# A 2-block transformer kernel: the first w_ada rows in three chunks, partly on TensorE, and four smaller moves

## The chip, the cores and the metric

The kernel runs on one core of a Trainium2 chip. The metric is the time of one execution on the device in microseconds (us), lower is better. A core has TensorE (PE), VectorE (DVE), ScalarE (ACT), GpSimd (POOL) and SyncE (SP); each has an instruction queue of its own, they meet by semaphores, and DMA queues move data between HBM and SBUF. Nearly all loads are issued by SP, in the order of its program.

## What is computed

The reference is two blocks, 256 tokens by 2048 features, in float32. What the change touches is the start of the first block and its three uses of the vector `mod`:

```python
c_act = jax.nn.silu(c)
mod = c_act @ w_ada[l] + b_ada[l]                 # 2048 x 12288
sh1, sc1, gt1, sh2, sc2, gt2 = jnp.split(mod, 6, axis=-1)
h = modulate(rms_norm(x, g_mix[l]), sh1, sc1)     # h * (1 + sc1) + sh1
z = h @ w_in[l]                                   # projections of both attentions, gates
...
x = x + gt1[:, None, :] * (merged @ w_out[l])
h = modulate(rms_norm(x, g_ffn[l]), sh2, sc2)
...
x = x + gt2[:, None, :] * y
```

`w_ada` has 100 MB. Only one token of `c` goes through it, so it is read once and never reused. The indexer of the second attention scores each key for each query over 16 heads of 64, and a top-64 picks keys. A second block (gated linear attention, SwiGLU) and the last norm follow.

## The kernel before

The kernel is written by hand, engine by engine, and the order on each queue is the order of the program. Every large product is made from **halves**: two k-tiles (256 rows) by 512 columns of a weight, 512 KB, loaded by SP into one of eight places of `raw`. ScalarE copies a half rounded to fp32r into one of four places of `whi` (L1041), VectorE subtracts and writes the rest into `wlo` (L1617), and TensorE does twelve matmuls with it (L499 to L501: high by high, high by low part of the weight, low part of the activation by high). `split` and `half` are these steps; `body` on ScalarE and VectorE runs ahead of TensorE by up to four halves, and small steps hang on it as hooks by the index of a half: after the split of that half, in order.

**Stage A** is the first 112 halves, 14 groups of 512 columns of `z`. It needs sh1 and sc1 per feature. Features come in 16 k-tiles; a pair of k-tiles feeds one half. The first six k-tiles (`EARLY`) are made before stage A: 16 row pieces of `w_ada` (128 rows by 2 x 768 columns, 768 KB each, `early_piece`, L329) are loaded into six slots; VectorE multiplies each by its column of `cact` = silu(c) and adds it to `acc0` (`early_add`, L1700). TensorE then sums over the 128 partitions by narrow matmuls with ones (`first_columns`, L577), in two chunks of columns (`CHUNKS`), VectorE makes `gs_mix` and `sh_mix` from that (`first_modulation`), and ScalarE and VectorE scale the transposed x and split it into `hi` and `lo` (`first_high`, `first_affine`, `first_low`, `first_pair`). x itself is loaded after four row pieces (L358); its root mean square is made on ScalarE and VectorE, its rows are scaled on ScalarE (L1074), and TensorE transposes them in eight pairs (`turn`, L524, L533). While TensorE would wait, `keep_running` gives it matmuls that nothing uses (L589).

Stage A runs over all 14 groups with the first three pairs, and then over them again with the other five. The last ten k-tiles come from 32 late pieces (640 KB, `late_piece`, L336), one after each half 4 to 35 in SP's queue; VectorE adds them (`late_add`, L1721), and after half 38 (`LATE_SUMMED`) 20 narrow matmuls sum them (L583). The pairs are made at `LATE_PAIRS`. All halves of `w_in` are loaded after all early pieces. Small vectors (later parameters, the bias table) are loaded after early piece 9 and transposed by TensorE before stage A (L572, L575).

The rest of `w_ada` is loaded in 128 chunks between later halves and added on VectorE (`ada_add`). Two of its results, the gates gt1 and gt2, are rows: `ada_rows` (L553) sums `ada_acc` over partitions and spreads it by four matmuls of float32 ones, once in stage U, once at the end of the first FFN. VectorE adds the bias (`modulation_row`).

In stages O, U, F1e, GQ, GO and F2p TensorE transposes eight pairs each between halves, one pair after a half (`turn`), and ScalarE and VectorE split each (`plain_pair`, `scaled_pair`, `held_pair`). In stage C1 the index heads run between halves: `ix_turn` of pair p after half 3p, `ix_scores` after half 3p + 2 (L687 to L710).

Of the kernel before, what the change touches and what calls it, by code (L numbers as in the profile page):

```python
# [5 lines left out]
P = 128  # L6
S = 256
TB = S // P
D = 2048
# [51 lines left out]
CHUNKS = ((0, 2), (2, EARLY), (EARLY, KT))  # L61
EARLY_ROWS = KT + 1
# [5 lines left out]
A_HELD = 3  # L68
A_ENDS = [A_FIRST + (KT // 2 - A_PAIRS) * (n + 1) for n in range(GROUPS)]
A_HALVES = [(g, p) for g in A_GROUPS for p in range(A_PAIRS)] + [(g, p) for g in A_AGAIN for p in range(A_PAIRS, KT // 2)]  # L70
LATE_SUMMED = 38
LATE_PAIRS = 41
# [19 lines left out]
def build_program(nc, A, out):  # L92
# [22 lines left out]
    ada0 = at("ada0", [P, SLOTS, 2 * EARLY * P], ARENA)  # L115
# [40 lines left out]
    gt_row1 = at("gt_row1", [P, D], ARENA + 48 * KB)  # L156
    xT1 = at("xT1", [P, KT, S], ARENA + 24 * KB)
# [96 lines left out]
    csg = small[:, 96:112]  # L254
    ss, ssy = small[:, 112:114], small[:, 114:116]
# [43 lines left out]
    def _(sp):  # L299
# [64 lines left out]
        for i in range(A_ENDS[-1]):  # L364
            first_half(i)
            if RING <= i < RING + 2 * KT:
                late_piece(i - RING)
            if i == 2 * RING:
                sp.wait_ge(sem("erow_held"), 1)
                sp.dma_start(e_dram, erow[:]).then_inc(sem("e_out"), 16)  # L370
# [111 lines left out]
    def _(pe):  # L482
# [23 lines left out]
        def group(it, phase, per, gper, idx0, gi, n, hooks, kt0=0, x_hi=hi, x_lo=lo, lead=None, parts=None, ready=None, ahead=4, made=None, by_block=None):  # L506
# [4 lines left out]
            for i in range(n):  # L511
# [8 lines left out]
                if lead is not None and i < 8 - ahead:  # L520
                    turn(lead, ahead + i, ready and (ready, (ahead + i) // 2 + 1))
                hooks(idx0 + i)

        def turn(src, g, ready=None):  # L524
# [11 lines left out]
            pairs[0] += 1  # L536

# [28 lines left out]
        pe.wait_ge(sem("xs_made"), 2)  # L566
        for g in range(KT // 2):
            turn(X, g)
        pe.wait_ge(sem("tt_free"), KT // 2)
        pe.wait_ge(sem("par_in"), 8 * 16)  # L570
        for n, rws in ((1, 120), (2, 116)):
            m = pe.transpose(aux[2][:, n % 2 * P:n % 2 * P + rws], parr[0:rws, n, :], ident[0:rws, 0:rws])  # L572
        m.then_inc(sem("par_T"), 1)
        pe.wait_ge(sem("rel_in"), 32)
        pe.matmul(aux[3][0:NH, :], relb[:], onehot[:], start=True, stop=True).then_inc(sem("par_T"), 1)  # L575

        def first_columns(n):  # L577

            k0, k1 = CHUNKS[n]
            acc, c0, w, wide = (acc1, 0, KT - EARLY, WIDE // 4) if n == 2 else (acc0, k0 * P, k1 - k0, WIDE // 2)  # L580
            for j in range(2 * w):
                c = c0 + j % w * P
                m = pe.matmul(aux[n % 2][:, j * wide:(j + 1) * wide], acc[:, j // w, c:c + P], ones[:, 0:wide], start=True, stop=True)  # L583
# [7 lines left out]
        pe.wait_ge(sem("ada0_sum"), KT - 3)  # L591
        keep_running(3)
        pe.wait_ge(sem("ada0_sum"), KT - 1)
        keep_running(1)
        for kc in range(2):
            pe.wait_ge(sem("ada0_sum"), KT + kc)
            first_columns(kc)
        keep_running(1)
        pe.wait_ge(sem("par_cols"), 2)
        pe.wait_ge(sem("erow_held"), 1)  # L600
# [18 lines left out]
        def sb_turn(h):  # L619
# [5 lines left out]
            pe.wait_ge(free0, 2 + GROUPS - A_HELD + (2 if h < NH // 2 else 5))  # L625
            pe.wait_ge(free1, 2 + GROUPS - A_HELD + (2 if h < NH // 2 else 5))
# [18 lines left out]
        def sb_values(h):  # L645
            pe.wait_ge(sem("sb_a"), h + 1)
            pe.wait_ge(sem("head_out"), h)
            if h == 0:
                pe.wait_ge(free0, 2 + GROUPS - A_HELD + 3)
                pe.wait_ge(free1, 2 + GROUPS - A_HELD + 3)  # L650
# [4 lines left out]
        for i, (g, p) in enumerate(A_HALVES):  # L655
            again = i >= A_FIRST
            n = (i - A_FIRST) // (KT // 2 - A_PAIRS) if again else i // A_PAIRS
            held = n < A_HELD if again else n >= GROUPS - A_HELD
            banks = first_banks[(GROUPS - A_HELD + n) % 3] if again and held else lin[n % 2] if again else first_banks[n % 3]
            if p == (A_PAIRS if again else 0) and not (again and held):  # L660
                pe.wait_ge(free0, 12 + n if again else n)
                pe.wait_ge(free1, 12 + n if again else n)
            if n == 0:
                pe.wait_ge(sem("tt_lo"), p + 1)
            half(0, "A", A_ENDS[-1], i, 0, 2 * p, p == (0 if held or not again else A_PAIRS), p == (KT // 2 - 1 if held or again else A_PAIRS - 1),
                 banks=banks)
            if i == LATE_SUMMED:
                pe.wait_ge(sem("ada0_sum"), EARLY_ROWS + 2 * KT)
                first_columns(2)
            if i == A_ENDS[0] - 1:  # L670
                project_ix()
            if i == A_ENDS[0] + 2:
# [92 lines left out]
        def o_hooks(it):  # L765
            def run(idx):
# [3 lines left out]
                if c >= 0 and step < 2:  # L770
                    if c == 0 and step == 0:
                        pe.wait_ge(sem("head_out"), 2 * NH)
                    turn(merged, 2 * c + step, (sem("og_add1"), c + 1))
# [5 lines left out]
        def last_merged(idx):  # L779

            if idx in (2, 3):
                turn(merged, 4 + idx, (sem("og_add1"), 4))
# [1837 lines left out]
```

## Time and profile before

| | us |
|---|---|
| median of three runs (2665.74 to 2667.66) | 2667.6 |
| the profiled execution | 2666.06 |
| its span, first to last instruction | 2664.2 |
| TensorE busy | 2625.6 |
| first projection matmul starts at | 48.21 |

The span is what the profile shows of one execution; all rows below come from it. The page gives busy time by engine, the span in slices, the DMA queues and the chain of waits that ended last; the timeline gives single instructions in order of time. TensorE being busy means that its pipeline holds a matmul; the distance from one start to the next says how fast it goes.

### The profile page before, as it was taken

To read this page: it belongs to the slowest core of one execution; us is meant where nothing else is said; L and a number is where in the kernel's file an instruction comes from. 1 tells how busy PE (TensorE), PEld (TensorE's weight loads), DVE (VectorE), ACT (ScalarE), POOL (GpSimd) and SP (SyncE) were. 2 spreads that over 40 slices of the span, in tenths; PEclk is the share of its full clock that TensorE was granted. 3 is DMA by queue.
4 is the path that set the end of the run, shared out by engine and by line. 5 is a ranking of instruction groups with operands and counts; after the bars stand their busy time and mean duration, and the time that the engine had idled before them with its cause. 6 is when DMAs were issued, how large, how long until landed. Compare 5 with 4: busy or idle time off the path is not lost.

```text
span 2664.2 us, 33329 instructions
## 1 busy us (share of the span) xinstructions
PE 2625.6 (99%) x12045; PEld 2164.4 (81%) x12045; DVE 1798.2 (67%) x2072; ACT 1297.8 (49%) x1574; POOL 230.2 (9%) x164
## 2 busy tenths in 40 slices
PE   5999999999999999999999999999999999999999
PEld 3888887888888888888888887887888888888887
DVE  7978777878776677776766855677555555555554
ACT  4455544455454444444444554556454444444443
POOL 0000000100000000000001210240001111111110
PEclk9999999999999999999999999999999999999999
DMA  9989768678867766666665666644666666666663
GB/s 382 401 308 340 243 209 281 196 237 283 304 211 241 220 220 219 218 218 216 218 195 177 198 178 181 190 143 132 199 186 193 190 189 189 190 190 191 191 191 134
DMA packets 280792, 585.61 MB, mean 220 GB/s; under 512 B 22033, under 2 KB 24493, under 8 KB 279797
## 3 DMA queue, kind: packets, MB, share of 16 engines
q1 hardware_dynamic: 280340, 583.61, 68.1%
q8 instruction: 58, 0.95, 0.1%
q10 hardware_dynamic: 352, 0.71, 0.1%
q14 instruction: 42, 0.34, 0.0%
HBM read 582.07 MB, written 2.11 MB: 219 GB/s over the span
## 4 chain that ended last, share of the span: by engine, by line
PE 96%; DVE 2%; DMA 1%; ACT 0%; issue 0%; DVEq 0%; ACTq 0%
PE lin L499 30%; PE lin L501 30%; PE lin L500 30%; DMA sb_ada<-in_w_ada_dram 1%; PE aux L812 1%; PE aux L499 1%; PE aux L501 1%; PE aux L500 1%; PE aux L533 1%; PE aux L986 0%; PE aux L823 0%; DVE sb_wlo L1617 0%; DVE sb_acc L1708 0%; PE aux L557 0%; PE aux L999 0%
## 5 line engine op out<-in xcount | busy, mean ns | idle before, releaser
L1617 DVE TENSOR_TENSOR sb_wlo<-sb_raw,sb_whi 128x1024 fp32r<-128x1024 f32 x896 | 1114.8, 1247 | 784.8 <-ACT sb_whi L1041 781.2
L1041 ACT ACTIVATE sb_whi<-sb_raw 128x1024 fp32r<-128x1024 f32 x896 | 948.9, 1060 | 1237.2 <-PE lin L501 1159.1
L499 PE MATMUL lin<-sb_whi,sb_act_hi 128*128 128x512 f32 x2620 | 1038.4, 396 | 1.9 <-DVE sb_wlo L1617 1.0
L501 PE MATMUL lin<-sb_whi,sb_act_lo 128*128 128x512 f32 x2620 | 1021.8, 390 | 0.0
L500 PE MATMUL lin<-sb_wlo,sb_act_hi 128*128 128x512 f32 x2620 | 1020.7, 390 | 0.0
L499 PEld LDWEIGHTS lin<-sb_whi,sb_act_hi 128*128 128x128 f32 x2620 | 492.5, 188 | 108.5 <-issue 9.3
L501 PEld LDWEIGHTS lin<-sb_whi,sb_act_lo 128*128 128x128 f32 x2620 | 492.1, 188 | 104.3
L500 PEld LDWEIGHTS lin<-sb_wlo,sb_act_hi 128*128 128x128 f32 x2620 | 492.7, 188 | 99.9 <-issue 1.9
L499 PE MATMUL lin<-sb_whi,sb_hid_hi 128*128 128x512 f32 x704 | 275.3, 391 | 0.0
L501 PE MATMUL lin<-sb_whi,sb_hid_lo 128*128 128x512 f32 x704 | 274.1, 389 | 0.0
L500 PE MATMUL lin<-sb_wlo,sb_hid_hi 128*128 128x512 f32 x704 | 274.0, 389 | 0.0
L501 PEld LDWEIGHTS lin<-sb_whi,sb_hid_lo 128*128 128x128 f32 x704 | 132.1, 188 | 27.6
L499 PEld LDWEIGHTS lin<-sb_whi,sb_hid_hi 128*128 128x128 f32 x704 | 132.2, 188 | 27.0
L500 PEld LDWEIGHTS lin<-sb_wlo,sb_hid_hi 128*128 128x128 f32 x704 | 132.2, 188 | 26.9
L1636 DVE SCALAR_TENSOR_TENSOR sb_ada_acc<-sb_ada_in,sb_small,sb_ada_acc 128x1024 f32<-128x1024 f32 x90 | 119.0, 1322 | 0.9 <-DVE sb_u_lo L1686 0.9
L2505 POOL TENSOR_TENSOR sb_yacc<-sb_yacc,sb_dstage 128x512 f32<-128x512 f32 x36 | 57.2, 1590 | 555.4 <-ACT sb_dstage L1055 555.4
L2505 POOL TENSOR_TENSOR sb_x<-sb_x,sb_dstage 128x512 f32<-128x512 f32 x36 | 63.6, 1766 | 336.2 <-ACT sb_dstage L1055 336.2
L2484 POOL TENSOR_TENSOR sb_hank<-sb_hank,sb_selneg 128x384 f32<-128x384 f32 x8 | 11.6, 1491 | 496.2 <-DVE sb_selneg L1895 496.2
L2511 POOL TENSOR_TENSOR sb_ubuf<-sb_ubuf,sb_cacc 128x512 f32<-128x512 f32 x11 | 18.1, 1648 | 397.4 <-ACT sb_ubuf L1055 397.4
L499 PE MATMUL lin<-sb_whi,sb_u_hi 128*128 128x512 f32 x128 | 51.0, 398 | 0.0
L501 PE MATMUL lin<-sb_whi,sb_u_lo 128*128 128x512 f32 x128 | 49.9, 390 | 0.0
L500 PE MATMUL lin<-sb_wlo,sb_u_hi 128*128 128x512 f32 x128 | 49.9, 390 | 0.0
(362 smaller groups left out, 1819.5 us busy)
## 6 DMA issues: line engine op xcount, KB each, us to landing
sb_raw<-in_w_in_dram SPq DMA_DIRECT2D x176, 512.0 KB, 6.7
sb_raw<-in_ffn_w_gu_dram SPq DMA_DIRECT2D x176, 512.0 KB, 3.7
sb_ada_in<-in_w_ada_dram SPq DMA_DIRECT2D x128, 512.0 KB, 5.1
sb_raw<-in_gla_w_in_dram SPq DMA_DIRECT2D x96, 512.0 KB, 3.8
sb_raw<-in_w_gate_dram SPq DMA_DIRECT2D x88, 512.0 KB, 3.8
sb_raw<-in_w_up_dram SPq DMA_DIRECT2D x88, 512.0 KB, 4.4
sb_raw<-in_w_down_dram SPq DMA_DIRECT2D x88, 512.0 KB, 4.4
sb_raw<-in_ffn_w_down_dram SPq DMA_DIRECT2D x88, 512.0 KB, 3.6
```

Of the source, the lines that this page charges most:

```text
L499: pe.matmul(o, h, whi[:, w], start=first and q == 0, stop=False)
L500: pe.matmul(o, h, wlo[:, w], start=False, stop=False)
L501: m = pe.matmul(o, l, whi[:, w], start=False, stop=last and q == 1)
L533: m = pe.transpose(aux[n % 4][:, q * S + tb * P:q * S + (tb + 1) * P], src[:, tb, (2 * g + q) * P:(2 * g + q + 1) * P], ident)
L812: m = pe.transpose(aux[f // 2][:, f % 2 * S + tb * P:f % 2 * S + (tb + 1) * P], src[:, tb, f * P:(f + 1) * P], ident)
L1041: act.activation(whi[:, idx % RING * HALF:(idx % RING + 1) * HALF], raw[:, idx // 2 % RING, idx % 2 * HALF:(idx % 2 + 1) * HALF], ACT.Copy ...
L1617: dve.tensor_tensor(wlo[:, c], raw[:, idx // 2 % RING, idx % 2 * HALF:(idx % 2 + 1) * HALF], whi[:, c].bitcast(fp32), ALU.subtract).then_i ...
L1636: dve.scalar_tensor_tensor(acc[:, c], ada_in[place][:], cact[:, kt:kt + 1], acc[:, c], ALU.mult, ALU.add).then_inc(sem("ada_sum"), 1)
L2484: pool.tensor_tensor(hank[:, h, :], hank[:, h, :], selneg[:], ALU.add).then_inc(sem("bias_made"), 1)
L2505: pool.tensor_tensor(y[:, 0, s], y[:, 0, s], dstage[:, c % 2, :], ALU.add).then_inc(sem("dstage_free"), 1)
L2511: pool.tensor_tensor(ubuf[:, 0, :], ubuf[:, 0, :], cacc[:].rearrange("p a t -> p (a t)")[:, 0:NB], ALU.mult).then_inc(sem("up_mul"), 1)
```

## The change

It does five things.

1. The early rows come in three chunks of two k-tiles: 48 row pieces of 128 rows by 2 x 256 columns (256 KB, rows of 1 KB), in six slots. 25 of them are multiplied by TensorE itself (`row_columns`: four matmuls with a column of `cact`, summed in PSUM), 23 are added by VectorE (`row_add`) and brought in by `chunk_columns`. x is loaded first of all; its scaling is shared by ScalarE and VectorE. The pieces of chunks two and three stand in SP's queue between the first halves (`PIECES_FROM`), and their takers between the first halves of TensorE (`ROWS_BEHIND`) and VectorE (`ADDS_AT`). Piece n waits until row n - 6 is taken. The first nine halves go by pair (three groups with pair 0, then with pair 1, then with pair 2). Late pieces stand after halves 7 to 38, and the late sums after half 39. The fillers before stage A are gone.
2. The later parameters are loaded after half 8 and transposed after half 12 of stage A.
3. The gate rows: `ada_acc` is split by ScalarE (`gate_high`) and VectorE (`gate_low`) into two fp32r parts; `ada_rows` makes eight fp32r matmuls.
4. `turn_two` turns two pairs after one half where two halves had one pair each.
5. `ix_scores` of pair p comes with `ix_turn` of pair p + 1, one half later.

The core of the diff:

```diff
+ROW_PIECES = 3 * KT
+TENSOR_ROWS = [n for n in range(KT) if n % 3 != 2] + list(range(KT + 1, 2 * KT, 2)) + [33, 36, 39, 42, 45, 47]
+VECTOR_ROWS = [n for n in range(ROW_PIECES) if n not in TENSOR_ROWS]
+ROWS_BEHIND = {0: (17, 19), 1: (21, 23), 2: (25, 27), 3: (29, 31), 4: (33,), 5: (36,), 6: (39, 42, 45, 47)}
+ADDS_AT = {0: (16, 18), 1: (20, 22), 2: (24, 26, 28, 30), 3: (32,), 4: (34, 35), 5: (37, 38, 40, 41), 6: (43, 44, 46)}
+PIECES_FROM = (0, 8, 16, 24, 32, 37, 42, 48)
+LATE_FROM = 7
-LATE_SUMMED = 38
-LATE_PAIRS = 41
+LATE_SUMMED = 39
+LATE_PAIRS = 42
...
+        def row_piece(n):
+
+            if n >= SLOTS:
+                row_taken(n - SLOTS)
+            kt, c = n % KT, n // KT
+            sp.dma_start(ada0[:, n % SLOTS, :].rearrange("p (b n) -> p b n", b=2), w_first[kt * P:(kt + 1) * P, :, 2 * c * P:2 * (c + 1) * P]
+                         ).then_inc(sem(f"ada0_in{n % SLOTS}"), 16)
+
+        def row_taken(n):
+
+            if n in TENSOR_ROWS:
+                sp.wait_ge(sem("ada0_T"), row_on_tensor(n))
+            else:
+                sp.wait_ge(sem("ada0_sum"), VECTOR_ROWS.index(n) + 1)
...
+        sp.dma_start(X[:], tokens(A["x"][0])).then_inc(sem("x_in"), 16)
+        for n in range(PIECES_FROM[1]):
+            row_piece(n)
+        for i in range(A_ENDS[-1]):
+            first_half(i)
+            if i + 2 < len(PIECES_FROM):
+                for n in range(PIECES_FROM[i + 1], PIECES_FROM[i + 2]):
+                    row_piece(n)
+            if i == 8:
                 for n, r, src in later_loads:
...
+        def row_columns(n):
+
+            kt, c = n % KT, n // KT
+            pe.wait_ge(sem(f"ada0_in{n % SLOTS}"), 16 * (n // SLOTS) + 16)
+            if all(m >= n for m in TENSOR_ROWS if m // KT == c):
+                pe.matmul(column_banks[c][:, 0:4], ident, nothing, start=True, stop=False)
+            for j in range(4):
+                m = pe.matmul(column_banks[c][:, j:j + 1], ada0[:, n % SLOTS, j * P:(j + 1) * P], cact[:, kt:kt + 1], start=False, stop=False)
+            m.then_inc(sem("ada0_T"), 1)
+
+        def chunk_columns(c):
+
+            pe.wait_ge(sem("ada0_sum"), sum(n < (c + 1) * KT for n in VECTOR_ROWS))
+            for j in range(4):
+                b, k = j // 2, 2 * c + j % 2
+                m = pe.matmul(column_banks[c][:, j:j + 1], acc0[:, b, k * P:(k + 1) * P], ones[:, 0:1], start=False, stop=j == 3)
+            m.then_inc(sem("ada0_T"), 1)
...
+        pe.wait_ge(sem("csg_made"), 2)
+        for n in TENSOR_ROWS[:8]:
+            row_columns(n)
         pe.wait_ge(sem("xs_made"), 2)
         for g in range(KT // 2):
             turn(X, g)
+            if g in (1, 3, 5):
+                row_columns(TENSOR_ROWS[8 + g // 2])
+        chunk_columns(0)
...
+        for i, (g, p, a, first, last) in enumerate(A_HALVES):
...
+            for n in ROWS_BEHIND.get(i, ()):
+                row_columns(n)
+            if i in (A_HELD, 2 * A_HELD):
+                chunk_columns(i // A_HELD)
+            if p == made:
+                made += 1
+                pe.wait_ge(sem("tt_lo"), made)
+            half(0, "A", A_ENDS[-1], i, 0, 2 * p, first, last, banks=banks)
+            if i == 12:
+                late_parameters()
...
         def ada_rows(n):
-            pe.wait_ge(sem("ada_sum"), 64 * (n - 1))
+            pe.wait_ge(sem("mod_made"), 2 * n - 1)
             for j in range(4):
-                m = pe.matmul(aux[j][:], ones, ada_acc[:, j * NB:(j + 1) * NB], start=True, stop=True)
+                c = slice(j * NB, (j + 1) * NB)
+                pe.matmul(aux[j][:], ones_r[:], (gt_hi1, gt_hi)[n - 2][:, c], start=True, stop=False)
+                m = pe.matmul(aux[j][:], ones_r[:], gt_lo[:, c], start=False, stop=True)
...
         def ix_hooks(idx):
-            p, step = idx // 3, idx % 3
-            if p < NIX // 2 and step == 0:
+            p = idx // 3
+            if idx % 3 == 0 and 1 <= p <= NIX // 2:
+                ix_scores(p - 1, p - 1)
+            if idx % 3 == 0 and p < NIX // 2:
                 ix_turn(p, p)
-            if p < NIX // 2 and step == 2:
-                ix_scores(p, p)
...
+        row_add(2)
+        row_add(5)
+        norm_stats(0)
+        dve.tensor_scalar(X[:, 1, :], X[:, 1, :], rstd[:, 1:2], None, ALU.mult).then_inc(sem("xs_made"), 1)
+        for n in (8, 11, 14):
+            row_add(n)
...
+        def early_pair(g):
+            first_modulation(g)
+            dve.wait_ge(sem("gs_made"), g + 1)
+            if g < 2:
+                first_affine(g)
+            first_low(g, xaff[:, g, :, :] if g < 2 else xT[:, 2 * g:2 * g + 2, :])
...
+        for g in range(A_PAIRS):
+            hk.setdefault(A_HELD * g, []).append(lambda g=g: early_pair(g))
+        for i, adds in ADDS_AT.items():
+            for n in adds:
+                hk.setdefault(i, []).insert(len(hk.get(i, ())) - (i == 6), lambda n=n: row_add(n))
...
+            act.activation((gt_hi if n else gt_hi1)[:], ada_acc[:], ACT.Copy).then_inc(sem("mod_made"), 1)
...
+            dve.tensor_tensor(gt_lo[:], ada_acc[:], (gt_hi if n else gt_hi1)[:].bitcast(fp32), ALU.subtract).then_inc(sem("mod_made"), 1)
```

## Rows read from the trace of the kernel before

**Rows 1.** The page: busy time by engine; the chain that ended last, by engine.
```profile
PE 2625.6 (99%) x12045; PEld 2164.4 (81%) x12045; DVE 1798.2 (67%) x2072; ACT 1297.8 (49%) x1574; POOL 230.2 (9%) x164
...
PE 96%; DVE 2%; DMA 1%; ACT 0%; issue 0%; DVEq 0%; ACTq 0%
```

**Rows 2.** Timeline of TensorE, stage A: start us, us, engine, line, operation, out<-in, count.
```profile
30.33 5.57 PE L533 MATMUL aux<-sb_con,sb_x 128*128 128x128 f32 x32 [20.52 <-ACT sb_x L1074]
...
48.21 0.47 PE L499 MATMUL lin<-sb_whi,sb_act_hi 128*128 128x512 f32 x1 [0.32 <-DVE sb_act_lo L1752]
...
130.06 0.47 PE L499 MATMUL lin<-sb_whi,sb_act_hi 128*128 128x512 f32 x1
...
147.68 0.47 PE L499 MATMUL lin<-sb_whi,sb_act_hi 128*128 128x512 f32 x1
...
155.94 4.53 PE L583 MATMUL aux<-sb_con,sb_acc 128*128 128x16 f32 x40
...
160.72 0.63 PE L500 MATMUL lin<-sb_wlo,sb_act_hi 128*128 128x512 f32 x1
...
164.05 0.40 PE L499 MATMUL lin<-sb_whi,sb_act_hi 128*128 128x512 f32 x1
```

**Rows 3.** Windows: stretch, length, busy us of PE, PEld, DVE, ACT, POOL, clock, DMA, GB/s.
```profile
10.00:30.00 20.00, 0.00 (x0) 0.00 (x0) 16.08 (x13) 9.41 (x9) 0.00 (x0) 1.00 1.03 401
...
120.00:140.00 20.00, 20.00 (x86) 15.61 (x85) 18.51 (x14) 9.79 (x13) 0.00 (x0) 1.00 1.04 402
...
161.00:165.00 4.00, 4.00 (x13) 3.09 (x13) 1.92 (x2) 3.94 (x7) 0.00 (x0) 0.63 0.71 244
```

**Rows 4.** Waits in 48 to 165 us: us in total, times, longest.
```profile
ACT sb_whi L1041 <- DMA sb_raw<-in_w_in_dram: 46.5, 29, 2.1
```

**Rows 5.** Timeline of ScalarE in the head.
```profile
18.03 1.91 ACT L1062 ACTIVATE sb_junk<-sb_x 128x2048 f32<-128x2048 f32 x1 [7.65 <-DMA sb_x<-in_x_dram]
...
22.09 1.28 ACT L1069 ACT_TABLE_LOAD   x1
...
26.29 3.90 ACT L1074 ACTIVATE sb_x<-sb_x,sb_small 128x2048 f32<-128x2048 f32 x2 [0.23 <-DVE sb_small L1677]
```

**Rows 6.** Timeline of VectorE, its first add.
```profile
10.93 1.02 DVE L1705 TENSOR_SCALAR sb_acc<-sb_ada,sb_small 128x1536 f32<-128x1536 f32 x1 [0.27 <-DVEq L1698]
```

**Rows 7.** Groups by form, 0 to 48 us: busy us, mean ns, idle before.
```profile
L1041 ACT ACTIVATE sb_whi<-sb_raw 128x1024 fp32r<-128x1024 f32 x2 | 2.1, 1049 | 5.2 <-DMA sb_raw<-in_w_in_dram 5.2
...
L1617 DVE TENSOR_TENSOR sb_wlo<-sb_raw,sb_whi 128x1024 fp32r<-128x1024 f32 x1 | 1.2, 1224 | 0.0
L1116 ACT ACTIVATE sb_act_hi<-sb_xT,sb_small 128x256 fp32r<-128x256 f32 x2 | 1.1, 593 | 0.0
...
L1718 DVE SCALAR_TENSOR_TENSOR sb_acc<-sb_ada,sb_small,sb_acc 128x512 f32<-128x512 f32 x1 | 0.8, 752 | 0.1
```

**Rows 8.** DMA issues: out<-in, KB each, median us to landing (second FFN; output stores).
```profile
sb_raw<-in_ffn_w_down_dram SPq DMA_DIRECT2D x77, 512.0 KB, 3.6
...
out_dram<-sb_x SPq DMA_DIRECT2D x2, 256.0 KB, 2.3
```

**Rows 9.** Timeline of SP's queue in the head, two rows of its issues.
```profile
0.75 2.17 SPq L333 DMA_DIRECT2D sb_ada<-in_w_ada_dram  x4
...
18.17 0.56 SPq L361 DMA_DIRECT2D sb_parr<-in_b_ada_dram  x1
...
22.97 9.38 SPq L333 DMA_DIRECT2D sb_ada<-in_w_ada_dram  x6
```

**Rows 10.** Timeline of TensorE: the half behind a turn, and a gate row.
```profile
627.12 0.47 PE L499 MATMUL lin<-sb_whi,sb_act_hi 128*128 128x512 f32 x1
627.43 0.39 PE L500 MATMUL lin<-sb_wlo,sb_act_hi 128*128 128x512 f32 x1
...
706.80 3.59 PE L557 MATMUL aux<-sb_ada_acc,sb_con 128*128 128x512 f32 x8
```

**Rows 11.** Timeline of ScalarE in stage U: a split and the idle time before it.
```profile
692.49 1.06 ACT L1041 ACTIVATE sb_whi<-sb_raw 128x1024 fp32r<-128x1024 f32 x1 [1.66 <-PE lin L501]
```

More of the change, by code:

```diff
@@ L254, in build_program @@
     csg = small[:, 96:112]
+    nothing = small[:, 184:188]
     ss, ssy = small[:, 112:114], small[:, 114:116]
@@ L519, in group @@
                 half(it, phase, per, idx0 + i, gi, kt0 + 2 * i, i == 0, i == n - 1, x_hi, x_lo, by_block=by_block if i == n - 1 else None)
-                if lead is not None and i < 8 - ahead:
-                    turn(lead, ahead + i, ready and (ready, (ahead + i) // 2 + 1))
+                if lead is not None and i < 8 - ahead and i % at_once == 0:
+                    for g in range(ahead + i, ahead + i + at_once):
+                        turn(lead, g, ready and (ready, g // 2 + 1))
                 hooks(idx0 + i)
@@ L536, in turn, with turn_two @@
             pairs[0] += 1
+        def turn_two(src, g, ready=None):
+            for n in range(2):
+                turn(src, g + n, ready)
         def ada_columns(part):
@@ L565, in _, with late_columns @@
         pe.wait_ge(sem("par_cols"), 1)
[L566 to L583, printed above, removed]
+        column_banks = (lin[0][1], aux[0], aux[1], aux[1])
+        def row_columns(n):
[12 more added lines that the diff above has]
+            m.then_inc(sem("ada0_T"), 1)
+        def late_columns():
+            pe.wait_ge(sem("ada0_sum"), EARLY_ROWS + 2 * KT)
+            pe.wait_ge(sem("par_cols"), 2)
+            pe.wait_ge(sem("erow_held"), 1)
+            for j in range(2 * LATE):
+                c = j % LATE * P
+                m = pe.matmul(aux[1][:, j * (WIDE // 4):(j + 1) * (WIDE // 4)], acc1[:, j // LATE, c:c + P], ones[:, 0:WIDE // 4], start=True, stop=True)
             m.then_inc(sem("ada0_T"), 1)
@@ L654, in _ @@
         first_banks = (lin[1], lin[0], aux[2:4])
[L655 to L666, printed above, removed]
+        made = 0
+        for i, (g, p, a, first, last) in enumerate(A_HALVES):
+            n = a - A_DRAINS
+            banks = lin[n % 2] if n >= A_HELD else first_banks[a % 3]
+            if first and a >= 3:
+                pe.wait_ge(free0, A_DRAINS + 1 + n if n >= A_HELD else a)
+                pe.wait_ge(free1, A_DRAINS + 1 + n if n >= A_HELD else a)
+            for n in ROWS_BEHIND.get(i, ()):
[8 more added lines that the diff above has]
+                late_parameters()
             if i == LATE_SUMMED:
-                pe.wait_ge(sem("ada0_sum"), EARLY_ROWS + 2 * KT)
-                first_columns(2)
-            if i == A_ENDS[0] - 1:
+                late_columns()
+            if i == A_ENDS[0]:
                 project_ix()
-            if i == A_ENDS[0] + 2:
+            if i == A_ENDS[0] + 3:
                 wix_turn()
@@ L873, in at_end @@
                     pe.wait_ge(sem("gpad_made"), FB)
-                if idx in range(24, 28) and n == 0:
-                    turn(X, idx - 24, (sem("x_made"), (idx - 24) // 2 + 1))
+                if idx in (24, 26) and n == 0:
+                    turn_two(X, idx - 24, (sem("x_made"), (idx - 24) // 2 + 1))
             for k in range(2):
```

233 lines of the change are left out of this document (115 added, 118 removed).

## The prediction

> **What bounds the kernel now.** The page first: TensorE is busy for 99% of the span and 96% of the chain that ended last is its matmuls [rows 1]. So a change gains only where TensorE waits, or where its own work shrinks. The timeline of TensorE shows the one long wait: the first projection matmul starts at 48.21 [rows 2]. From there halves (12 matmuls, two k-tiles by 512 columns) follow without a gap: 30 halves up to 130.06, 2.72 us each. Half 36 starts at 147.68, and the 39th ends at 155.94, where the late columns begin; 39 times 2.72 would end at 154.3, so 1.7 us are lost in between.
>
> The windows say why [rows 3]: from 10 us to 140 us the DMA queues carry some 400 GB/s without a break. The waits say it again: ScalarE's splits wait 46.5 us in 29 pieces for `sb_raw` [rows 4]. So the head has two limits at once, the late start of TensorE and a full DMA queue. A half needs 0.52 MB, a late piece 0.66 MB; both together take 2.95 us at 402 GB/s, more than the 2.72 us of a half. The lead of the old order (eight halves loaded before TensorE starts) is used up by half 30.
>
> **The first rows, up to the first half.** x goes to the head of SP's queue. It landed at 18.03 behind 3.1 MB of rows [rows 5]; without them (7.9 us at 400 GB/s) about 10.1. Squares took 4.1, the table load 1.28 [rows 5], root, reciprocal and hand-overs 0.6; the scaling is shared by ScalarE and VectorE, 2.0 instead of 3.9. Rows of x are scaled at 18.3. TensorE however has eight rows of w_ada ahead of the transposes. A row is four narrow matmuls; the late columns are 20 of them, 40 records in 4.37 us [rows 2], so 0.87 a row. The first can start at 10.9, when silu(c) is there [rows 6]. Rows 0, 1, 3 and 4 are taken by 14.7; row 10's piece waits for row 4 (six slots), and lands behind pieces 6 to 9 and half 0 at about 19.3. Transposes start at 20.2; they took 5.6 [rows 2], three rows between them 2.6, the last copy 0.6 (somewhat over half of a split's 1.05): 29.0. Then the split of half 0 on ScalarE 1.05 and VectorE 1.2, the modulation 0.45, the high part 1.05, the low part 0.65 (half of VectorE's 1.2) [rows 7], hand-overs 0.4: first half at T0 = 33.8, 14.4 us earlier than before.
>
> **Halves 0 to 6: where I expect the time to go.** SP's queue is in order, and each row piece now waits for the row six earlier to be taken. Many of these takers stand behind a projection step: on VectorE behind a split, on TensorE behind a half. The halves' own loads stand in the same queue behind these waits. One load, from issue to landing, is 3.6 for 512 KB with little queued [rows 8]; for 256 KB I take 3.0, that less 0.6 for the bytes (ends: 2.3, the 256 KB stores of [rows 8], and 3.6). An issue is 0.5 [rows 9], a VectorE add of 512 columns 0.75 [rows 7]. In us from T0:
> - Row 16 is added after the first pair's modulation, at 0.2; only then are pieces 22 and 23 and half 2 issued. Row 23 lands at 4.0, so TensorE starts half 1 at 4.9, and after rows 25 and 27 half 2 at 9.4.
> - Piece 31 waits for row 25 (8.5), half 3 is behind it, lands at 13.2; split 2.3, modulation, high and low 2.5: half 3 at 18.0, though half 2 ended at 12.1.
> - Pieces 39 to 41 wait for row 33, which TensorE takes after half 3 (21.6); half 5 is behind them, lands 5.7 later and is split at 29.6: half 5 at 29.8, half 4 having ended at 24.3.
> - Piece 45 waits for row 39, taken after half 5 (33.4); pieces 46, 47 and half 6 are behind it: landed 39.1, split 41.4, three adds 43.5, column sums 44.8, modulation, first pair (1.7 on ScalarE), low: half 6 at 47.9.
>
> So half 6 starts at 81.7, against 48.21 + 6 x 2.72 = 64.5 before. DMA carries little meanwhile: about 19 MB by the time half 6 has landed (73 us), where the old order had carried 28.
>
> **The clock.** After the late columns the next eight matmuls came 0.43 apart instead of 0.23 until 164.05 [rows 2]: 1.2 GHz instead of 2.4 (granted clock 0.63 in that window [rows 3]), 1.7 us lost, with nothing before but narrow matmuls. Halves 0, 3, 5 and 6 start after narrow matmuls and a wait, and the fillers that ran ahead of half 0 are gone. If all four start low, the steps above come to 52.8 from T0 (half 0's loss is partly behind row 23's landing), half 6 itself losing 1.7 more. Without any loss it is 47.9; the row is nearest to a loss, but of 4.4 us of narrow matmuls. I take about a third of it.
>
> **From half 6 to the late columns.** Half 6's load is issued 12.8 ahead of half 6, at 69 us, and from there the queue can stay full: halves 6 to 39 and 32 late pieces are 38.8 MB, 96.5 us, so half 39 lands at 168, before TensorE wants it (171.5): no stall. TensorE does 34 halves (92.5), and the later parameters, moved from a hidden place into its stream after half 12: two transposes and one matmul, 1.3. Their ten small loads (4.8 of SP's time [rows 9]) now stand after half 8, ahead of late piece 1, which waits for row 43 anyway; that piece and the others move three halves back, which costs what the sum holds. The store of the bias row moves to half 32, far ahead of its reader. Late columns start at 175.5 without clock losses, 182.1 with all. Before, after 40 halves, they would be at 155.94 + 2.72 = 158.7. That is 16.8 to 23.4 us lost. One half less stands between the late columns and the first late pair (two halves, 5.4 us); modulation, pair and low part need about 3, so they stay hidden.
>
> **Gate rows.** Four matmuls in two passes each, 8 records in 3.4 us, twice [rows 10]. Eight fp32r matmuls of 512 columns at 0.23 each are 1.8: 1.6 saved, twice, 3.2. The split into high (ScalarE, 2.0, by the 2048-column copies of [rows 5]) and low (VectorE, 2.4, two of the 1.2 of [rows 7]) lies two halves ahead of its use, where ScalarE idles 1.66 per half [rows 11]. Behind them stand a split and two pairs on each engine, which are due a half later than they come; without that cover up to 4.4 each would show. No new DMA.
>
> **Two pairs at a time, index scores.** After a turn the first spacing is 0.31 instead of 0.23 [rows 10]; every break that goes saves that 0.08 or nothing. 15 turns and 8 index scores: 0 to 1.8, I take 1.3. The scores come one half later, and so do relu, sums and mask on ScalarE and VectorE; the eight top-8 steps end at the same half as before, so the attention that waits for them does not move.
>
> **The sum.** +16.8 +2.2 (a third of the clock) -0.5 (between the ends of the landing) -3.2 -1.3 = +14.0 on the profiled execution's 2666.06 (span 2664.2): 2680. That execution is 1.5 below the median of 2667.6, within 0.06%. With all waits short (256 KB at 2.3, T0 at 32, no clock loss) it is about 2672; with all clock losses 2685, with a landing of 3.6 near 2689.
>
> **A rule of the skill.** By the rows a 256 KB piece lands after about 3.0 [rows 8], estimated. The Trainium skill (DMA: Bandwidth & Descriptors, Rules for kernel authors) asks for 1 MiB or more per DMA, which speaks against pieces of a third of the old size; its fit (Anatomy of one DMA) of 2.0 us and bytes over 436 GB/s would make 2.6 of the 3.0, an estimate, and with four such landings on the chain the sum 1.6 lower, 2678. No row here shows a load of 256 KB alone.
>
> **Rivals.**
> 1. The queue stays full (faster). If takers are always ahead of the pieces, DMA sets the end as it did: half 36 was gated at 147.68; three more halves are 1.6 MB, 3.9 us, so half 39 runs at 151.6, and the late columns start at 154.3, 4.4 earlier than before's 158.7. With the gate rows and the breaks 2657. It decides if the queue never runs dry before half 6, that is if half 6 starts by about 62. For it: T0 plus 40 halves plus 14 rows is also 154. Against it: the order of the takers in the code, above all rows 33 and 39. Chance 0.13.
> 2. Only one of the stalls shows (no change). If halves 3 and 5 are not held up (10 us less) and only half 6 waits, with no clock loss: 2668. Chance 0.12.
> 3. My forecast, 2672 to 2688. 0.68.
> 4. More than that: 1 KB rows slower than the 2 KB ones, or a wait in the gate rows that shows; 2688 to 2695. 0.07.
> That the change doesn't do what it says is unlikely: each step is in the diff.
>
> About 0.2% (5.3 us) is what a measurement of this kernel can tell from no change. Faster is rival 1, 0.13; same rival 2, 0.12; slower the rest, 0.75. The range, 2664 to 2690, leaves out rival 1 and the far end of 4. The slower cases alone lie at 2672 to 2690.
>
> **What would show it.** Right: first half at 31 to 35; TensorE idle before halves 3 and 5 for 4 to 6 us each and before half 6 for over 10; DMA in 30 to 75 us well under 400 GB/s; SP waiting for `sb_ada` rows there; late columns at 172 to 183; gate rows 1.8 each. Wrong: half 6 before 68, or DMA near 400 GB/s throughout.

## The result, and the profile after

The changed kernel takes 2707.2 us (median of four runs, 2705.5 to 2708.5) against 2667.5 us, a ratio of 1.0151 with a 95% interval of 1.0139 to 1.0163. It is slower, as forecast, but by 40 us where 12 were forecast (14 against the profiled execution), and it lies outside the range (2664 to 2690). The profiled execution took 2706.84 us with a span of 2705.0, 40.8 more than the profiled one of before.

All of it is lost before the late columns. Starts in us; the late columns of before are set behind 40 halves, as in the change, and the forecast is the one without clock losses:

| | before | forecast | changed kernel |
|---|---|---|---|
| half 0 | 48.2 | 33.8 | 43.5 |
| half 3 | 56.6 | 51.8 | 66.0 |
| half 5 | 62.0 | 63.6 | 82.7 |
| half 6 | 64.7 | 81.7 | 105.0 |
| late columns | 158.7 | 175.5 | 201.3 |

The page of the changed kernel, busy time by engine and the chain that ended last by engine; both answer to [rows 1]:

```profile
PE 2663.5 (98%) x12241; PEld 2209.6 (82%) x12241; DVE 1798.9 (67%) x2085; ACT 1299.5 (48%) x1576; POOL 230.2 (9%) x164
...
PE 95%; DVE 3%; DMA 1%; ACT 1%; issue 1%; SPq 0%; ACTq 0%; DVEq 0%
```

TensorE is busy for 37.9 us more than before, so little of the 40.8 is idle time that was added on balance. The rows of w_ada alone are busy for 35.8 us, in the groups of 0 to 106 us (busy us, mean ns of one, idle before):

```profile
L638 PE MATMUL lin<-sb_small,sb_ada 128*128 128x1 f32 x88 | 18.9, 347 | 0.0
L638 PE MATMUL aux<-sb_small,sb_ada 128*128 128x1 f32 x112 | 16.9, 278 | 1.9 <-DMA sb_ada<-in_w_ada_dram 1.9
```

At the 0.87 of the forecast these 25 rows would be 21.8. The timeline of TensorE, stage A, of the changed kernel (start us, us, engine, line, operation, out<-in, count, idle before; compare [rows 2]) shows where they lie and what they cost:

```profile
12.67 13.79 PE L638 MATMUL lin<-sb_small,sb_ada 128*128 128x1 f32 x64
26.32 1.95 PE L588 MATMUL aux<-sb_con,sb_x 128*128 128x128 f32 x8
28.06 1.71 PE L638 MATMUL lin<-sb_small,sb_ada 128*128 128x1 f32 x8
...
39.97 3.55 PE L638 MATMUL aux<-sb_small,sb_ada 128*128 128x1 f32 x16
43.48 0.80 PE L553 MATMUL lin<-sb_whi,sb_act_hi 128*128 128x512 f32 x1
...
48.57 1.84 PE L638 MATMUL aux<-sb_small,sb_ada 128*128 128x1 f32 x16
...
66.02 0.80 PE L553 MATMUL lin<-sb_whi,sb_act_hi 128*128 128x512 f32 x1 [5.58 <-DVE sb_act_lo L1842]
...
82.70 0.80 PE L553 MATMUL aux<-sb_whi,sb_act_hi 128*128 128x512 f32 x1 [6.14 <-DVE sb_wlo L1714]
...
90.73 3.77 PE L638 MATMUL aux<-sb_small,sb_ada 128*128 128x1 f32 x16 [1.87 <-DMA sb_ada<-in_w_ada_dram]
100.03 1.87 PE L646 MATMUL aux<-sb_con,sb_acc 128*128 128x1 f32 x8 [5.52 <-DVE sb_acc L1806]
104.99 0.79 PE L553 MATMUL lin<-sb_whi,sb_act_hi 128*128 128x512 f32 x1 [3.10 <-DVE sb_act_lo L1842]
...
201.26 4.83 PE L656 MATMUL aux<-sb_con,sb_acc 128*128 128x16 f32 x40
```

A row of w_ada is eight records. The first eight rows take 13.79 us, 1.72 each; rows 17 and 19 ahead of half 0 take 3.5, and rows 21 and 23 behind it, the same work, 1.7 together (48.57 to 50.27, where half 1 starts). Transposes go the same way: 8 records in 1.74 from one start to the next, where the turn of two pairs between halves later takes 0.79 (734.86 to 735.65). And from 43.48 to 48.57 half 0 takes 5.1 instead of 2.72.

The windows of the changed kernel (columns as in [rows 3]):

```profile
11.00:48.00 37.00, 35.92 (x160) 34.82 (x160) 12.27 (x23) 15.47 (x20) 0.00 (x0) 1.00 0.61 190
...
75.00:100.00 25.00, 11.46 (x56) 10.11 (x54) 7.53 (x9) 2.11 (x2) 0.00 (x0) 0.65 0.65 206
...
105.00:109.60 4.60, 4.60 (x11) 3.63 (x12) 4.47 (x5) 1.99 (x3) 0.00 (x0) 0.50 1.04 408
120.00:140.00 20.00, 20.00 (x88) 15.70 (x87) 18.40 (x14) 10.03 (x14) 0.00 (x0) 1.00 1.03 401
```

DMA is down to 190 and 206 GB/s where before had some 400, and back at 401 from half 6 on. From 105 to 109.6 the granted clock is 0.50, that is 1.2 GHz, and the matmuls of half 6 start 0.43 apart.

Two views of the waits (us in total, times, longest): SP's queue for the takers of the rows, 0 to 106 us, and TensorE for what then comes late, 43 to 106:

```profile
SPq L378 <- PE lin L638: 21.4, 11, 7.0
SPq L378 <- PE aux L638: 15.1, 5, 6.2
SPq L378 <- DVE sb_acc L1808: 12.6, 2, 7.1
SPq L378 <- DVE sb_acc L1806: 11.9, 7, 6.4
```

```profile
PE lin L553 <- DVE sb_act_lo L1842: 8.7, 2, 5.6
PE aux L553 <- DVE sb_wlo L1714: 6.1, 1, 6.1
PE aux L646 <- DVE sb_acc L1806: 5.5, 1, 5.5
PE aux L638 <- DMA sb_ada<-in_w_ada_dram: 1.9, 1, 1.9
```

SP stands 61 us before row pieces (L378). TensorE idles before halves 3, 5 and 6, as forecast. The landings from 44 to 92 us (KB each, median us from issue), for [rows 8]:

```profile
sb_ada<-in_w_ada_dram SPq DMA_DIRECT2D x26, 256.0 KB, 4.1
sb_raw<-in_w_in_dram SPq DMA_DIRECT2D x7, 512.0 KB, 6.3
```

### The profile page after: what moved, and what is told of

Its sections match the earlier page's. It is cut to its first block, busy times and chain, and to the rows that moved or that the text cites. A ratio compares the mean times of both kernels' runs of the same rounds, so it can differ in the third digit from the quotient of the medians.

```text
span 2705.0 us, 33772 instructions
## 1 busy us (share of the span) xinstructions
PE 2663.5 (98%) x12241; PEld 2209.6 (82%) x12241; DVE 1798.9 (67%) x2085; ACT 1299.5 (48%) x1576; POOL 230.2 (9%) x164
## 4 chain that ended last, share of the span: by engine, by line
PE 95%; DVE 3%; DMA 1%; ACT 1%; issue 1%; SPq 0%; ACTq 0%; DVEq 0%
PE lin L553 29%; PE lin L555 29%; PE lin L554 29%; DVE sb_wlo L1714 1%; PE aux L588 1%; PE aux L898 1%; DMA sb_raw<-in_w_in_dram 1%; PE lin L638 1%; PE aux L553 1%; PE aux L555 1%; PE aux L554 1%; PE aux L1072 0%; PE aux L909 0%; DMA sb_gt_bias<-in_b_ada_dram 0%; PE aux L638 0%
## 5 line engine op out<-in xcount | busy, mean ns | idle before, releaser
L2603 POOL TENSOR_TENSOR sb_x<-sb_x,sb_dstage 128x512 f32<-128x512 f32 x36 | 63.6, 1767 | 336.2 <-ACT sb_dstage L1141 336.2
L2582 POOL TENSOR_TENSOR sb_hank<-sb_hank,sb_selneg 128x384 f32<-128x384 f32 x8 | 11.7, 1490 | 539.0 <-DVE sb_selneg L1987 539.0
```

Of the source, the lines that this page charges most:

```text
L2582: pool.tensor_tensor(hank[:, h, :], hank[:, h, :], selneg[:], ALU.add).then_inc(sem("bias_made"), 1)
L2603: pool.tensor_tensor(y[:, 0, s], y[:, 0, s], dstage[:, c % 2, :], ALU.add).then_inc(sem("dstage_free"), 1)
```

## The experiments

Two theories stood after the traces. **A, the queue:** six slots tie the halves' loads to the takers of rows. **B, the clock:** TensorE does rows, transposes and the first halves at 1.2 GHz. The runs on the head, in the order of what they explain (starts in us, from each one's profile; time is the median; the profiled execution of e2 took 2705.8, that of e3 2693.3):

| run | half 0 | half 6 | late columns | time |
|---|---|---|---|---|
| changed kernel | 43.5 | 105.0 | 201.3 | 2707.2 |
| e1 sixteen slots | 43.5 | 84.4 | 180.2 | 2687.2 |
| e5 halves ahead | 44.4 | 89.9 | 185.6 | 2692.8 |
| e2 fillers | 42.4 | 102.7 | 198.7 | 2714.2 |
| e3 slots and fillers | 50.4 | 91.0 | 186.6 | 2692.1 |
| e6 chunk 0 on VectorE | 31.1 | 72.6 | 168.8 | 2675.2 |
| e7 fewer rows | 30.7 | 67.5 | 164.4 | 2669.7 |
| e9 fewer rows, fillers | 30.6 | 65.0 | 159.7 | 2667.2 |
| before | 48.2 | 64.7 | 158.7 | 2667.5 |

**e1, sixteen slots** (ten more places in memory that is free then; the ten semaphores are borrowed from later loads).

```diff
-SLOTS = 6
+SLOTS = 16
-    ada0 = at("ada0", [P, SLOTS, 2 * 2 * P], ARENA + 24 * KB)
+    ada0 = at("ada0", [P, SLOTS, 2 * 2 * P], ARENA)
```

> The changed kernel with sixteen places for row pieces instead of six: a piece waits for the row sixteen earlier, so the loads of halves 2 to 6 no longer stand in SP's queue behind rows that TensorE or VectorE take after a half. Theory A (the queue: six slots tie the loads of the halves to the takers): half 0 stays at 43.5, the waits before halves 3, 5 and 6 go, half 6 starts at about 75 instead of 105, the late columns at about 169 instead of 201, and the time falls by some 32 us to about 2675. Theory B (the loss is mostly TensorE at its lower clock and the work of the rows themselves): the waits go only in part, the late columns come no earlier than 190, the time stays above 2695.

Measured: 2687.2, a ratio to before of 1.0074 (1.0059 to 1.0090), 20 us of the 40. The waits of the changed kernel before half 5 and for late adds are gone, half 6 is 20.6 earlier, and the late columns 21.0. Theory A is shown, for half of the loss. What stays, in the timeline of TensorE of e1, is the slow first stretch, unchanged, and two waits of another kind:

```profile
39.58 0.57 PE L637 MATMUL aux<-sb_small,sb_con 128*128 128x4 f32 x2
40.01 3.55 PE L639 MATMUL aux<-sb_small,sb_ada 128*128 128x1 f32 x16
...
62.40 0.79 PE L554 MATMUL lin<-sb_whi,sb_act_hi 128*128 128x512 f32 x1 [2.43 <-DVE sb_act_lo L1843]
...
84.42 0.80 PE L554 MATMUL lin<-sb_whi,sb_act_hi 128*128 128x512 f32 x1 [3.09 <-DVE sb_act_lo L1843]
```

Both follow the column sums of a chunk: modulation, the pair's scaling and its low part are on VectorE and ScalarE, and TensorE has nothing to do meanwhile. I had counted on 75 for half 6; these waits, the slow halves 0 and 3 and the 4.3 us of four rows ahead of half 6 stand in between.

**e5, halves ahead of the pieces** (six slots).

```diff
-PIECES_FROM = (0, 8, 16, 24, 32, 37, 42, 48)
+PIECES_FROM = (0, 8, 16, 16, 16, 16, 16, 16, 16, 48)
```

> The changed kernel, six slots, with one thing moved in SP's queue: the loads of halves 1 to 7 stand ahead of row piece 16 instead of between the pieces of chunks two and three. This splits the queue theory in two. If what counts is that the loads of halves 3, 5 and 6 themselves stand behind waiting row pieces, their splits are done early, the wait of 6.1 us before half 5 goes, that before half 3 shrinks, and half 6 starts some 15 us earlier than 105; the time falls to about 2692. If what counts is that with six slots the rows of chunks two and three themselves come too late (each piece is issued only when the row six before is taken, and lands some 3 to 6 us later), half 6 stays within 6 us of 105 and the time at 2700 or more.

Measured: 2692.8, ratio 1.0098 (1.0083 to 1.0114), and half 6 at 89.9: the first of the two. So of the 20 us that the slots give, 14 come from the halves' own loads standing behind pieces that wait for a taker; only the other 6 need more slots. A load that is due sooner stood in an in-order queue behind one that must wait.

**e2, fillers ahead of and between the first rows** (six slots), and **e3**, the same with sixteen slots.

```diff
+        pe.wait_ge(sem("out_done"), 16)
+        keep_running(3)
         pe.wait_ge(sem("par0_in"), 6 * 16)
...
+        keep_running(1)
         pe.wait_ge(sem("csg_made"), 2)
         for n in TENSOR_ROWS[:8]:
             row_columns(n)
+            if TENSOR_ROWS.index(n) % 2 == 1:
+                keep_running(1)
```

> The changed kernel with matmuls of 512 columns that nothing uses: three before the first transpose, one before the rows, one after every second of the first eight rows; still six slots. Theory B (the head is late because TensorE runs rows and transposes at the lower clock: 1.72 us a row where one between halves takes 0.85): rows fall to 0.85 us, half 0 starts at about 34 instead of 43.5 although the fillers take 3.4 us themselves, and it takes 2.7 instead of 5.1; the waits before halves 3, 5 and 6 remain, the time falls by 8 to 12 us to about 2697. If the slow rows are not the clock but a price of narrow matmuls on freshly landed pieces, rows stay at 1.7, half 0 comes at 46 and the time rises by about 3 us.

> Both edits together: sixteen slots and the fillers. If the two losses are separate they add: half 0 at about 34, half 6 at about 63, late columns at about 157 (before had 158.7 for the same half), time about 2665, the level of the kernel before. If with a full queue the transfers set the pace (402 GB/s), halves wait for their loads again and the time stays at 2670 to 2680.

Measured: e2 2714.2 (2705.8 to 2715.3), ratio 1.0177 (1.0161 to 1.0192); e3 2692.1 (2685.3 to 2693.3), ratio 1.0084 (1.0068 to 1.0099): no gain, a loss of 5 to 7 in the medians. The timeline of TensorE in e2, whose profiled execution is the fastest of the four:

```profile
13.56 1.93 PE L645 MATMUL lin<-sb_small,sb_ada 128*128 128x1 f32 x16
15.35 1.10 PE L669 MATMUL lin<-sb_con 128*128 128x512 f32 x2
16.29 1.84 PE L645 MATMUL lin<-sb_small,sb_ada 128*128 128x1 f32 x16
17.99 1.97 PE L669 MATMUL lin<-sb_con 128*128 128x512 f32 x2
19.76 3.41 PE L645 MATMUL lin<-sb_small,sb_ada 128*128 128x1 f32 x16
...
31.70 0.98 PE L645 MATMUL lin<-sb_small,sb_ada 128*128 128x1 f32 x8
```

The first four rows cost 0.9 each, so the price of 1.72 is TensorE's clock and not the piece or the narrow shape: that part of theory B is shown. But from 18 to 31 rows and fillers take twice as long again, with a filler behind every second row, and the granted clock there is 0.50; from 31.70 on a row costs 0.8 once more. In the profile of e3, with the same fillers, the clock stays at 0.50 from 18 to 43, and the row at the same place is slow:

```profile
34.99 1.71 PE L646 MATMUL lin<-sb_small,sb_ada 128*128 128x1 f32 x8
```

So half 0 starts at 42.4 in the one profile and at 50.4 in the other. The spread of the times fits this: the mean granted clock of the profiled execution of e2 is 0.988 and that of its other three, 8 to 10 us longer, 0.985; e3 has 0.992 in its fastest execution (2685.3) and 0.989 in the other three. A difference of 0.003 over some 2700 us is 8.1 us. As a remedy the fillers failed: in both traces the clock falls among the first rows in spite of them, and they add their own time. That the clock makes the whole spread is not shown, as each kernel has one trace.

**e6, the first chunk on VectorE** (sixteen slots).

```diff
-TENSOR_ROWS = [n for n in range(KT) if n % 3 != 2] + list(range(KT + 1, 2 * KT, 2)) + [33, 36, 39, 42, 45, 47]
+TENSOR_ROWS = [0, 1, 3, 4] + list(range(KT + 1, 2 * KT, 2)) + [33, 36, 39, 42, 45, 47]
...
-        for n in TENSOR_ROWS[:8]:
+        for n in TENSOR_ROWS[:4]:
             row_columns(n)
...
-            if g in (1, 3, 5):
-                row_columns(TENSOR_ROWS[8 + g // 2])
...
-        for n in (8, 11, 14):
+        for n in range(6, KT):
             row_add(n)
```

> Sixteen slots as in e1, and of the first chunk only rows 0, 1, 3 and 4 on TensorE; the other twelve are added by VectorE, which idled for 12.7 us before the first split; so no row stands between the transposes. If the price of rows on a TensorE at 1.2 GHz sets the first half, transposes start at about 20 and take about 6 us as in the kernel before, half 0 starts at 31 to 33 instead of 43.5, and as the rest is that of e1 the time is about 2676 (2687 less 11). If instead the landing of the rows sets it, half 0 moves by less than 4 us.

Measured: 2675.2, ratio 1.0030 (1.0018 to 1.0042), half 0 at 31.1. Twelve us go with seven rows that TensorE no longer does; the engine that takes them had been idle. The timeline of TensorE in e6:

```profile
12.91 6.96 PE L639 MATMUL lin<-sb_small,sb_ada 128*128 128x1 f32 x32
19.73 5.07 PE L589 MATMUL aux<-sb_con,sb_x 128*128 128x128 f32 x32
27.34 1.05 PE L647 MATMUL lin<-sb_con,sb_acc 128*128 128x1 f32 x8 [2.54 <-DVE sb_acc L1805]
...
31.06 0.77 PE L554 MATMUL lin<-sb_whi,sb_act_hi 128*128 128x512 f32 x1
```

Without rows between them the 32 transposes take 5.07, much as in [rows 2]; TensorE even waits 2.5 for VectorE's last add.

**e7, fewer rows on TensorE in chunks two and three** (the diff is against e6).

```diff
-TENSOR_ROWS = [0, 1, 3, 4] + list(range(KT + 1, 2 * KT, 2)) + [33, 36, 39, 42, 45, 47]
+TENSOR_ROWS = [0, 1, 3, 4] + [17, 19, 21, 23] + [33, 36, 39, 42]
...
+ROWS_BEHIND = {1: (17,), 2: (19, 21), 3: (23,), 4: (33,), 5: (36,), 6: (39, 42)}
+ADDS_AT = {0: (16, 18, 20, 22), 1: (24, 25, 26, 27), 2: (28, 29, 30, 31), 3: (32, 34, 35, 37), 4: (38, 40, 41, 43), 5: (44, 45), 6: (46, 47)}
```

> As e6, and of the second and third chunk only four rows each on TensorE (12 and 12 on VectorE, where 8 and 10 were). A row between halves costs TensorE 0.85 us and an add costs VectorE 0.75 beside splits of 1.2 a half. If TensorE is what the halves wait for, half 6 follows half 0 after some 34 us instead of 41 and the time is about 2669, near the kernel before; if VectorE becomes the bound in the two chunks, nothing is gained over e6 (2676).

Measured: 2669.7, ratio 1.0010 (1.0000 to 1.0019); from half 0 to half 6 36.8 instead of 41.6. Four rows fewer stand between them, 3.5 of the 4.8 us at 0.87: rows between halves are on the path that sets the end.

**e9, e7 with fillers in the waits**, and **e10**, with e8's bias load as well.

```diff
+        keep_running(2, lin[0][0])
         chunk_columns(0)
+        keep_running(2, lin[0][0])
...
             if i in (A_HELD, 2 * A_HELD):
+                if i == 2 * A_HELD:
+                    keep_running(1, aux[0])
                 chunk_columns(i // A_HELD)
+                keep_running(2 if i == A_HELD else 3, aux[1] if i == A_HELD else aux[0])
```

> e7 with matmuls of 512 columns that nothing uses in TensorE's waits: two before and two behind the column sums of the first chunk, two behind those of the second, one before and three behind those of the third. In e7 half 0 took 4.8 us, half 3 4.0 and the halves from 6 on lost 3.0, where 2.7 a half is usual: some 6.5 us at 1.2 GHz. If the waits behind narrow matmuls are what drops the clock, wide matmuls in them keep it: half 6 starts at about 63 instead of 67.5, and the time is about 2664. If they come too late or cost what they save, as in e2, the time stays at 2668 to 2671.

> e9 with the early load of the bias row from e8. e8 gained 1.3 us on e4; so about 2662.7 if e9 comes out at 2664, below both kernels and level with e8 (2664.1); 2668 if the fillers do nothing.

Measured: e9 2667.2, ratio 1.0001 (0.9992 to 1.0010); e10 2665.8, ratio 0.9997 (0.9988 to 1.0006). Windows of e7, then of e9, from 30 to 75 us:

```profile
30.00:50.00 20.00, 16.84 (x83) 14.44 (x84) 15.48 (x24) 4.94 (x6) 0.00 (x0) 0.84 0.99 317
50.00:75.00 25.00, 21.53 (x94) 17.99 (x94) 19.19 (x24) 8.61 (x11) 0.00 (x0) 0.73 1.04 375
```

```profile
30.00:50.00 20.00, 18.75 (x103) 15.40 (x103) 17.58 (x27) 4.87 (x6) 0.00 (x0) 1.00 1.09 360
50.00:75.00 25.00, 23.54 (x112) 17.98 (x112) 19.39 (x24) 11.12 (x15) 0.00 (x0) 1.00 1.05 381
```

The granted clock is 1.00 throughout in e9 and 0.84 and 0.73 in e7, and half 6 comes 2.5 earlier and the late columns 4.6. So here the fillers hold the clock, as they did not in e2. They stand in waits here, and behind fewer narrow matmuls; which of the two counts was not tested. The gain in time is 2.4 us where 5.7 were expected: fillers and waits for VectorE's adds take some, and the late columns themselves take 5.7 (159.74 to 165.43) instead of 4.4 in e7.

e10 is 1.4 below e9, much as e8 is below e4, and can't be told from before.

e9 also shows what holds the idea back in this form. It has half 0 17.7 us earlier than before, a full clock and only 2 us of waits between halves 0 and 6, and yet half 6 starts 0.3 later than before. Six halves take 16.3 of the 34.5 us in between; eight rows, two column sums, the two chains of modulation behind them and their fillers take the rest. What before did on VectorE while TensorE had nothing to do is now in TensorE's stream.

**e4, the old head with the rest of the change** (gate rows in two parts, two pairs a turn, index scores moved; the diff is that of the change without its first part and the later parameters), and **e8**, e4 with the bias row loaded early:

```diff
-    gt_bias1 = at("gt_bias1", [P, D], ARENA + 24 * KB)
+    gt_bias1 = at("gt_bias1", [P, D], 64 * KB)
...
-                if (it, s) == (0, 6):
-                    sp.wait_ge(sem("tt_T"), KT)
+                if (it, s) == (0, 5):
+                    sp.wait_ge(half_used, H0["U"])
```

> The kernel before with only the later parts of the change: gate rows in two parts, two pairs a turn, index scores moved; the head with the 16 early pieces as before. From the positions of the halves in the changed trace (its lead over before after stage A shrinks from 42.4 to 40.6) these parts together are worth 1.7 us, so about 2665.8. By the terms of my prediction (3.2 for the gate rows, 1.3 for the breaks) it would be 2663. In its trace VectorE should again hold up TensorE by 0.9 us after the first gate row, behind the load of the bias row, and by about 0.6 us behind the second.

> e4 (old head, new rest) with the row of the bias for the first gate loaded to a place that is free after stage O, so that the load no longer waits for the last transposes of the attentions' output. If the wait of VectorE for that load takes back most of what the first gate row gains, VectorE's wait of over 4 us goes, TensorE's wait of 0.9 us behind it goes, and the trace gains 0.9 us on e4 from there on; the time falls to about 2664.6, which a timing can hardly tell from e4 but the trace can. If VectorE's own work is the bound, the wait stays.

Measured: e4 2665.5, ratio 0.9992 (0.9983 to 1.0001); e8 2664.1, ratio 0.9989 (0.9980 to 0.9998). e8 is the only kernel of this study that is faster than before beyond its interval, by 3 us. The first gate row on VectorE, in the changed kernel and then in e8:

```profile
756.57 2.48 DVE L2067 TENSOR_TENSOR sb_gt_row<-aux,sb_gt_bias 128x512 f32<-128x512 f32 x4 [4.64 <-DMA sb_gt_bias<-in_b_ada_dram]
```

```profile
709.14 2.48 DVE L1996 TENSOR_TENSOR sb_gt_row<-aux,sb_gt_bias 128x512 f32<-128x512 f32 x4
```

VectorE waits 4.64 us for the bias in the changed kernel (4.70 in e4) and not at all in e8. TensorE's waits for splits, from 660 us on, in the kernel before, in e4 and in e8:

```profile
PE lin L499 <- DVE sb_wlo L1617: 1.0, 3, 0.6
```

```profile
PE lin L503 <- DVE sb_wlo L1638: 2.5, 5, 0.9
```

```profile
PE lin L503 <- DVE sb_wlo L1638: 1.6, 4, 0.6
```

Of the 1.2 us that the faster first gate row saves (3.03 from 706.80 to the next half before, 1.81 after), 0.9 came back as a wait of TensorE, as the bias came no sooner; e8 removes it.

## Why the prediction was wrong

The direction, the place and the waits (takers behind halves, the halves' loads behind them) were right; the clock of the head was not in the working, and the sum, +14.0, missed +40.8 by 26.8. By its steps:

- **"The first rows, up to the first half": T0 = 33.8 failed, by 9.7.** This is the step that the miss begins with. I priced a row at 0.87, from the late columns, which run right behind halves at the high clock, and the transposes at the 5.6 of before. In the head nothing but narrow matmuls and transposes runs, and a row costs 1.72 [rows 2 has both spacings, 0.43 and 0.23, which I used only for halves]. The first row also starts 1.8 later than 10.9, 1.35 of it because the small parameters land later (10.72, before 9.37). By parts: the transposes start at 26.3 and not at 20.2 (6.1), they and the three rows between them take 11.7 and not 8.2 (3.5), and the column sums of the first chunk, which the step leaves out, take 1.6; what follows is 1.5 shorter. e2 shows the price to be the clock, e6 that these rows set the start of half 0.
- **"The clock": mis-sized.** Halves 0, 3, 5 and 6 lost 2.4, 2.6, 1.6 and 2.4, together 9.0 (each half's length less 2.72). I had taken 2.2, a third of the 6.6 that all four came to in my working. All four started low, three of them for longer than that. That is 6.8 of the miss.
- **"Halves 0 to 6": right in its order, short in its landings.** Half 3 waits behind piece 31, half 5 behind 41, half 6 behind 47, as written. But from the taking of the row that frees the piece to the landing of the half I had 4.7, 5.7 and 5.7 us; it took 7.4, 7.5 and 7.4 (half 6: row 39 taken at 87.9, landed at 95.3). A 256 KB piece lands after 4.1 us, not 3.0, outside my ends of 2.3 and 3.6, and the loads of halves 3, 5 and 6 after 6.9, 5.9 and 5.8, not 3.6. Why they land later than those of [rows 8] is not shown; the loads of halves 5 and 6 were each issued right behind three pieces. With the 0.5 that I took off, 6.7. The chain that ended last, for half 6 (start us, us, what):

```profile
87.19 0.80 PE aux L638 x8
...
89.44 5.83 DMA sb_raw<-in_w_in_dram
95.29 1.06 ACT sb_whi L1127
```

- **"From half 6 to the late columns"** held: 93.8 forecast, 96.3 measured, the difference being half 6's clock, counted above. The later parameters cost 1.25 (126.42 to 127.67), 1.3 forecast.
- **"Gate rows": -3.2 forecast, -0.8 measured.** Each row takes 1.8 (749.35 to 751.16) instead of 3.0 as the gap between halves has it (I had taken the 3.4 of the pipeline's busy time), so 2.4 together; 0.9 and 0.7 come back as TensorE's waits for splits, as VectorE has the same sums to do and, for the first, waits for the bias. I had looked for what the added split delays, not for what had been hidden by the slow rows.
- **"Two pairs at a time, index scores": -1.3 forecast.** The breaks that go save 0.9 for the fifteen turns (two single turns and their halves 22.74 from 626.53 to 649.27, one double 22.65) and 0.65 for the eight score steps. But "the attention that waits for them does not move" failed: the end of the selection on VectorE comes 0.8 later than the shift of its neighbours, and TensorE's halves behind it lose 0.8. Its last step on VectorE, before and then changed:

```profile
495.94 0.56 DVE L1895 TENSOR_TENSOR sb_selneg<-sb_selneg,sb_con 128x384 f32<-128x384 f32 x1
```

```profile
538.77 0.56 DVE L1987 TENSOR_TENSOR sb_selneg<-sb_selneg,sb_con 128x384 f32<-128x384 f32 x1
```

That is 42.8 later, where the halves before it stand 42.0 later and those behind it 42.8. Together the parts behind the late columns gain 1.7 instead of 4.5. The remaining 0.8 of the 26.8 is spread over rows at a low clock and roundings.

Rival 1 (a full queue, 2657) fell with 206 GB/s from 75 to 100 us, and would not have come even so: in e9 the queue carries 360 to 402 GB/s and TensorE's own stream sets the end. Rival 4 was the nearest: slower pieces and waits behind the gate rows did come, but its price was too small. My bounds were those of single terms; the clock was a term of every step of the head, and I had bounded it only for halves.

On the rule of the Trainium skill (DMA: Bandwidth & Descriptors; Anatomy of one DMA): its fit, which the page gives for DMAs issued by GpSimd and which the prediction took for loads of SP, comes to 2.6 us for a piece of 256 KB, an estimate, and the trace has 4.1; for 512 KB it comes to 3.2, and the trace has 6.3 in this stretch. The measurement decides. Whether larger pieces, as its Rules for kernel authors ask, would do better in this place was not tried.

## What to carry to other kernels

Price an operation at the clock of the place it moves to: look for a stretch of the same kind of work in the same company, and if there is none, take both levels as the ends of its price. A load that an engine needs soon must not stand in an in-order queue behind one that waits for that engine. And before moving work to an engine's idle time, check whether another engine idles there too, at a better price.

## What the runs showed of the hardware

- From 12.67 to 43.5 us TensorE issued narrow matmuls and transposes almost without a gap, busy 35.92 of the 37 us from 11 to 48, and stayed at 1.2 GHz; the spacing fell from 0.43 to 0.23 only in half 0, at 48.3. The Trainium skill (TensorE: Matmul & The Clock Gate, Part 1) has the clock follow TensorE's recent activity; the busy time of the profile is no measure of that in this trace.
- The clock column reads 1.00 for 11 to 48 us, where the spacings are those of the stretch from 105.0 to 109.6 with 0.50; the trace holds no record of the clock before the rise at 48.3. At the start of this span the spacing is to be trusted, not the column.
- Loads of 256 and 512 KB took 4.1 and 6.3 us to land in the stretch from 44 to 92 us, in which DMA carried 187 GB/s on average and not 400.
